# Hybrid decoder layer on one core: both feed-forwards begin with four plain hidden chunks instead of two, and the bias of x is added piece by piece inside the second norm

## What is computed

```
def _swiglu(x, w_gu, w_down):
    gate, up = jnp.split(x @ w_gu, 2, axis=-1)
    return (jax.nn.silu(gate) * up) @ w_down

h = _layernorm(ALPHA * x + 0.5 * _swiglu(x, p['ffa_w_gu'], p['ffa_w_down']), p['ln1_g'], p['ln1_b'])
...
h = _layernorm(ALPHA * h + mix, p['ln2_g'], p['ln2_b'])
y = _layernorm(ALPHA * h + 0.5 * _swiglu(h, p['ffb_w_gu'], p['ffb_w_down']), p['ln3_g'], p['ln3_b'])
```

## Time and profile before

| | us |
|---|---|
| median of 3 runs | 1262.5 (1261.45 to 1262.73) |
| the profiled execution, its own time | 1261.35 |
| its span (first to last instruction) | 1259.6 |
| TensorE busy | 1197.3 |
| VectorE busy | 842.0 |
| ScalarE busy | 498.2 |

### The profile page before, as it was taken

How to read it: one execution, slowest core, us unless ns; L and a number is a source line. 1 busy time by engine, 2 the same in 40 slices (tenths; PEclk the granted TensorE clock), 3 DMA queues, 4 the chain that set the end, 5 groups by cost and what they waited for, 6 DMA issues and landing times.

```text
span 1259.6 us, 30052 instructions
## 1 busy us (share of the span) xinstructions
PE 1197.3 (95%) x12778; PEld 1076.6 (85%) x12778; DVE 842.0 (67%) x1187; ACT 498.2 (40%) x759; POOL 89.7 (7%) x89
## 2 busy tenths in 40 slices
PE   9899999999999999998888988999799999999996
PEld 7899999999999988885546445698689999999996
DVE  6985895798467445164645543787796698579854
ACT  5441443254244325233433424333643244225433
POOL 0000000000020200000540021010000000000011
PEclk9999999999999999999999999999899999999998
DMA  5233222232315657646654898741123232422311
GB/s 206 98 96 123 101 93 93 101 107 95 112 63 178 237 169 250 219 143 200 220 175 154 272 301 286 255 169 60 42 97 94 102 120 68 132 95 101 101 34 69
DMA packets 56726, 177.41 MB, mean 141 GB/s; under 512 B 7185, under 2 KB 7442, under 8 KB 47250
## 3 DMA queue, kind: packets, MB, share of 16 engines
q1 hardware_dynamic: 53426, 169.48, 39.4%
q10 hardware_dynamic: 3168, 6.02, 1.4%
HBM read 164.64 MB, written 10.83 MB: 139 GB/s over the span
## 4 chain that ended last, share of the span: by engine, by line
PE 77%; DVE 10%; SPq 4%; issue 3%; DMA 2%; ACT 2%; POOL 1%; ACTq 0%; DVEq 0%; POOLq 0%
PE banks L585 30%; PE banks L385 30%; SPq L3057 2%; PE banks L1970 2%; PE banks L1227 2%; PE banks L408 2%; PE banks L977 2%; PE banks L1522 1%; PE banks L2040 1%; SPq L3049 1%; PE banks L2235 1%; DVE y_sum L1161 1%; DVE weights_lo L364 1%; DVE x_sums_lo L506 1%; PE banks L2227 1%
## 5 line engine op out<-in xcount | busy, mean ns | idle before, releaser
L364 DVE TENSOR_TENSOR weights_lo<-weights_raw,weights_hi 128x1024 fp32r<-128x1024 f32 (+1 forms) x82 | 96.5, 1183 | 119.7 <-ACT weights_hi L356 119.2
L356 ACT ACTIVATE weights_hi<-weights_raw 128x1024 fp32r<-128x1024 f32 (+1 forms) x82 | 82.4, 1013 | 189.8 <-PE banks L385 172.5
L385 PE MATMUL banks<-hidden_hi,weights_hi 128*128 128x260 f32 x576 | 116.3, 283 | 0.0
L385 PE MATMUL banks<-hidden_hi,weights_lo 128*128 128x260 f32 x576 | 115.5, 282 | 0.0
L385 PE MATMUL banks<-hidden_lo,weights_hi 128*128 128x260 f32 x576 | 115.5, 282 | 0.0
L585 PE MATMUL banks<-x_sums_hi,more_weights_hi 128*128 128x260 f32 x352 | 100.4, 285 | 0.7 <-DVE more_weights_lo L561 0.7
L585 PE MATMUL banks<-x_sums_hi,more_weights_lo 128*128 128x260 f32 x352 | 99.9, 284 | 0.0
L585 PE MATMUL banks<-x_sums_lo,more_weights_hi 128*128 128x260 f32 x352 | 99.9, 284 | 0.0
L385 PEld LDWEIGHTS banks<-hidden_hi,weights_hi 128*128 128x128 f32 x576 | 88.7, 188 | 0.3
L385 PEld LDWEIGHTS banks<-hidden_hi,weights_lo 128*128 128x128 f32 x576 | 88.7, 188 | 0.0
L385 PEld LDWEIGHTS banks<-hidden_lo,weights_hi 128*128 128x128 f32 x576 | 88.5, 188 | 0.0
(11 more groups left out here) (412 smaller groups left out, 3188.0 us busy)
## 6 DMA issues: line engine op xcount, KB each, us to landing
cache_pages<-in_cache_k SPq DMA_DIRECT2D x128, 256.0 KB, 3.6
weights_raw<-in_gate_up_b SPq DMA_DIRECT2D x22, 1024.0 KB, 4.7
weights_raw<-in_gate_up_a SPq DMA_DIRECT2D x21, 1024.0 KB, 4.7
cache_pages<-in_cache_v SPq DMA_DIRECT2D x64, 256.0 KB, 3.6
weights_raw<-in_w_in SPq DMA_DIRECT2D x13, 1024.0 KB, 6.3
projected<-in_cache_v SPq DMA_DIRECT2D x48, 256.0 KB, 3.6
weights_raw<-in_down_a SPq DMA_DIRECT2D x8, 896.0 KB, 4.5
weights_raw<-in_down_b SPq DMA_DIRECT2D x8, 896.0 KB, 4.6
```

What stands on the lines that cost most here:

```text
L356: nc.scalar.activation(WH[pr.slot(i, k)][:, 0:nk, :], RAW[slot][:, 0:nk, P * (k % 2):P * (k % 2) + P], ACT.Copy).then_inc(split_hi, 1)
L364: nc.vector.tensor_tensor(WL[pr.slot(i, k)][:, 0:nk, :], RAW[slot][:, 0:nk, P * (k % 2):P * (k % 2) + P], WH[pr.slot(i, k)][:, 0:nk, :].bi ...
L385: mm = nc.tensor.matmul(acc[s][:, a, 0:HALF], w[slot][:, t, :], x[:, k0 + t, HALF * a:HALF * a + HALF], start=begins and t == tiles[0] and ...
```

## The change

`PLAIN` becomes `(4, 4)`, one number for each feed-forward. `up_a` and `up_b` run twice, so that each feed-forward begins with four plain chunks and has three pairs left in its first group. For this case there is a new order of ACT's and DVE's lists, `longer_begin_scalar` and `longer_begin_vector`, which weaves the second plain product, the sums of x and the first pair's weights. The sums of x are rounded in the order 0, 1, 2, 3 rather than 1, 2, 0, 3. In the second norm `plain_x_scalar` adds the bias to one piece of `y_sum` at a time: three pieces after the norm's fourth `biased_scalar`, then one behind each, the last after the norm. The first sum of x, which reads the chunks 0 to 3 alone, waits for seven pieces, the others for all eleven.

```diff
-PLAIN = 2
+PLAIN = (4, 4)
...
-    def feed_forward(up, pair0):
+    def feed_forward(u, up, pair0):
...
-            first = PLAIN if not at else 0
+            first = PLAIN[u] if not at else 0
...
-    up_a = Product(PAIR_BODY, 1)
-    sevens_a, downs_a = feed_forward(up_a, 0)
+    up_a = Product(PAIR_BODY, PLAIN[0] // 2)
+    sevens_a, downs_a = feed_forward(0, up_a, 0)
...
-    up_b = Product(PAIR_BODY, 1, outp, LATE_RING)
-    sevens_b, downs_b = feed_forward(up_b, FC - PLAIN)
+    up_b = Product(PAIR_BODY, PLAIN[1] // 2, outp, LATE_RING)
+    sevens_b, downs_b = feed_forward(1, up_b, FC - PLAIN[0])
...
+        X_PIECES = ((0, 0), (1, 0), (2, 0), (0, 1), (1, 1), (2, 1), (3, None), (4, None), (5, None), (6, None), (7, None))
...
-        def plain_x_scalar(act):
-
-            act.wait_ge(x_ready, DC + 22)
-            for c in range(DC):
-                bias = VEC[:, V_LN + 3 * DC + c:V_LN + 3 * DC + c + 1]
-                nc.scalar.activation(Y[:, c, :], Y[:, c, :], ACT.Identity, bias=bias).then_inc(g("x_passes"), 1)
+        def plain_x_scalar(act, e):
+
+            c, h = X_PIECES[e]
+            act.wait_ge(x_ready, DC + 11 + e + 1)
+            bias = VEC[:, V_LN + 3 * DC + c:V_LN + 3 * DC + c + 1]
+            out = Y[:, c, :] if h is None else Y[:, c, HALF * h:HALF * h + HALF]
+            nc.scalar.activation(out, out, ACT.Identity, bias=bias).then_inc(g("x_passes"), 1)
 
         def x_sum_vector(dve, u, n):
 
             out = XS[:, n, :, :]
             if u:
-                dve.wait_ge(g("x_passes"), 4 + DC)
+                dve.wait_ge(g("x_passes"), 4 + (7 if n == 0 else len(X_PIECES)))
...
-        def plain_silu_scalar(act, up, k):
-            act.wait_ge(slab_used, up.slab(0, k) + 1)
+        def plain_silu_scalar(act, up, i, k):
+            act.wait_ge(slab_used, up.slab(i, k) + 1)
+            if i:
+                act.wait_ge(acc_free[2 + k], up.set_uses(i - 1, k + 2) + 1)
             nc.scalar.activation(halves(SCR[:, k, :]), accv(k), ACT.Silu).then_inc(acc_free[k], 1)
...
+        def longer_begin_scalar(act, up, u, sv):
+            for k in range(2):
+                split_high(act, up, 1, k)
+                plain_silu_scalar(act, up, 0, k)
+                x_sum_high(act, u, k)
+            for k in range(2, 4):
+                split_high(act, up, 1, k)
+            for n in range(2, 4):
+                x_sum_high(act, u, n)
+            for c in range(2):
+                plain_high_scalar(act, up, 0, c)
+            outer_high(act, sv, 0)
+            for k in range(2):
+                plain_silu_scalar(act, up, 1, k)
+            for which in ("first", "last"):
+                sums_high(act, sv, 0, which)
+            for c in range(2):
+                plain_high_scalar(act, up, 1, c)
+
+        def longer_begin_vector(dve, up, u, sv):
+            for k in range(2):
+                x_sum_vector(dve, u, k)
+            split_low(dve, up, 1, 0)
+            plain_hidden_vector(dve, up, 0, 0)
+            split_low(dve, up, 1, 1)
+            plain_hidden_vector(dve, up, 0, 1)
+            for n in range(2, 4):
+                x_sum_vector(dve, u, n)
+            for k in range(2, 4):
+                split_low(dve, up, 1, k)
+            for n in range(2):
+                x_sum_low(dve, u, n)
+            for c in range(2):
+                plain_low_vector(dve, u, 0, c)
+            outer_sums_vector(dve, sv, 0)
+            whole_sum_vector(dve, sv, 0)
+            outer_low(dve, sv, 0)
+            for n in range(2, 4):
+                x_sum_low(dve, u, n)
+            for which in ("first", "last"):
+                sums_low(dve, sv, 0, which)
+            plain_hidden_vector(dve, up, 1, 0)
+            outer_sums_vector(dve, sv, 1)
+            whole_sum_vector(dve, sv, 1)
+            plain_hidden_vector(dve, up, 1, 1)
+            for c in range(2):
+                plain_low_vector(dve, u, 1, c)
+
...
+
+        def feed_forward_scalar(act, up, u, sevens, downs):
+            if up.times > 1:
+                longer_begin_scalar(act, up, u, sevens[0])
+            else:
+                begin_scalar(act, up, u, sevens[0])
...
-        def norm_scalar(act, n, following=None):
+        def norm_scalar(act, n, following=None, plain=False):
...
                 biased_scalar(act, n, e)
                 if following and e == 4:
                     split_high(act, following, 0, 3)
+                if plain:
+                    for before in range(3) if e == 3 else (e - 1,):
+                        plain_x_scalar(act, before)
...
-            load_weights(sp, up_b, 0, by_pair(gu_b))
+            for i in range(up_b.times):
+                load_weights(sp, up_b, i, by_pair(gu_b))
...
-            norm_scalar(act, 1, up_b)
-            plain_x_scalar(act)
+            norm_scalar(act, 1, up_b, True)
+            plain_x_scalar(act, len(X_PIECES) - 1)
...
             multiply_halved(pe, up_b, 1)
+            for i in range(1, up_b.times):
+                multiply(pe, up_b, i, XH, XL)
```

More of the change, by code:

```diff
@@ L426, in layer @@
         COMBINE = {"second": 1, "third": 2, "ends": 3, "gates": 4, "hidden": 5}
-        X_STEP = {("sum", 0): 1, ("sum", 1): 2, ("sum", 2): 3, ("sum", 3): 4, ("low", 1): 5, ("low", 2): 6, ("low", 0): 7, ("low", 3): 8}
-        X_PASS = {1: 1, 2: 2, 0: 3, 3: 4}
+        X_STEP = ({("sum", 0): 1, ("sum", 1): 2, ("sum", 2): 3, ("sum", 3): 4, ("low", 1): 5, ("low", 2): 6, ("low", 0): 7, ("low", 3): 8},
+                  {(what, n): 4 * (what == "low") + n + 1 for what in ("sum", "low") for n in range(4)})
+        X_PASS = ({1: 1, 2: 2, 0: 3, 3: 4}, {0: 1, 1: 2, 2: 3, 3: 4})
         WEIGHT_AT = {4: 0, 1: 1, 2: 2, 5: 3, 6: 4, 7: 5, 3: 6}
@@ L456, in x_step @@
         def x_step(u, kind, n):
-            return 8 * u + X_STEP[kind, n]
+            return 8 * u + X_STEP[PLAIN[u] > 2][kind, n]
         def x_part(c, h):
@@ L756, in feed_forward_scalar, with begin_vector @@
             sums_high(act, sv, 0, "last")
-            for c in range(PLAIN):
-                plain_high_scalar(act, up, u, c)
+            for c in range(2):
+                plain_high_scalar(act, up, 0, c)
+        def begin_vector(dve, up, u, sv):
+            x_sum_vector(dve, u, 0)
+            x_sum_vector(dve, u, 1)
+            outer_sums_vector(dve, sv, 0)
+            whole_sum_vector(dve, sv, 0)
+            x_sum_vector(dve, u, 2)
+            x_sum_vector(dve, u, 3)
+            outer_low(dve, sv, 0)
+            sums_low(dve, sv, 0, "first")
+            plain_hidden_vector(dve, up, 0, 0)
+            for n in (1, 2):
+                x_sum_low(dve, u, n)
+            plain_hidden_vector(dve, up, 0, 1)
+            sums_low(dve, sv, 0, "last")
+            for n in (0, 3):
+                x_sum_low(dve, u, n)
[3 more added lines that the diff above has]
+            whole_sum_vector(dve, sv, 1)
@@ L769, in feed_forward_vector @@
         def feed_forward_vector(dve, up, u, sevens, downs):
-            sv = sevens[0]
-            x_sum_vector(dve, u, 0)
-            x_sum_vector(dve, u, 1)
-            outer_sums_vector(dve, sv, 0)
-            whole_sum_vector(dve, sv, 0)
-            x_sum_vector(dve, u, 2)
-            x_sum_vector(dve, u, 3)
-            outer_low(dve, sv, 0)
-            sums_low(dve, sv, 0, "first")
-            plain_hidden_vector(dve, up, u, 0)
-            for n in (1, 2):
-                x_sum_low(dve, u, n)
-            plain_hidden_vector(dve, up, u, 1)
-            sums_low(dve, sv, 0, "last")
-            for n in (0, 3):
-                x_sum_low(dve, u, n)
-            for c in range(PLAIN):
-                plain_low_vector(dve, u, c)
-            outer_sums_vector(dve, sv, 1)
-            whole_sum_vector(dve, sv, 1)
+            if up.times > 1:
+                longer_begin_vector(dve, up, u, sevens[0])
+            else:
+                begin_vector(dve, up, u, sevens[0])
             for n, (sv, down) in enumerate(zip(sevens, downs)):
@@ L3075, in _ @@
             sp.dma_start(RAW[1][:, :, :], by_pair(gu_a)(0, 1)).then_inc(raw_ready[1], 16)
+            for i in range(1, up_a.times):
+                load_weights(sp, up_a, i, by_pair(gu_a))
             load_feed_forward(sevens_a, downs_a, gu_a, down_a)
@@ L3220, in _ @@
             multiply(pe, up_a, 0, XH, XL, (x_ready, 0))
+            for i in range(1, up_a.times):
+                multiply(pe, up_a, i, XH, XL)
             feed_forward_tensor(pe, 0, sevens_a, downs_a)
@@ L3272, in by_pair, with gate_up @@
         return w[0].reshape(DC, P, -1, 2 * P).transpose(2, 1, 0, 3).reshape(-1, P, DC * 2 * P)
-    def gate_up(w):
+    def gate_up(w, plain):
         whole = w[0].reshape(DC, P, 2, FC // 2, 2 * P).transpose(3, 2, 1, 0, 4).reshape(FC, P, DC * 2 * P)
```

48 lines of the change are left out of this document (30 added, 18 removed).

## The result

The changed kernel takes 1245.76 us (median of 4 runs, 1240.84 to 1248.71), the kernel before beside it 1261.97 (1259.47 to 1262.73). The ratio is 0.9871, with a 95% interval of 0.9844 to 0.9899: faster by 1.0 to 1.6%. The median lies 0.9 us under the lower end of the predicted range, 1246.7. The profiled execution took 1248.23, its span is 1246.4; from the profiled execution before that is 13.1 us (13.2 in span), against a forecast of 14.1.

What follows compares the result with a forecast made beforehand. TensorE's matmuls plus its stalls and slow stretches were taken to bound the kernel. First feed-forward -1.2 and second -12.9 (norm's +0.5 included) gave -14.1 us, a median of 1248.4; the 8-in-10 range was 1246.7 to 1253.

Steps and rivals of the forecast that it cites:

- What bounded the kernel: Whole kernel: TensorE, busy for 95% of the span, sets the time by its matmuls plus where it stands or runs slowly.
- S: Second feed-forward, end of first plain product to down product: 66.70 us before, forecast 53.8 with the norm's 0.5, -12.9.
- Where the 16.3 us were: Second feed-forward's loss over 420 matmuls: waits of 8.6 and 2.4 us, most of the rest the low clock.
- the two waits: TensorE in the second feed-forward: 8.6 us for the first pair's outer low weights, 2.4 for the second pair's sums.
- The lists keep up: VectorE and ScalarE ready before TensorE asks, so no stalls from first plain product to down product: 53.3 us per feed-forward.
- The tightest margin: Second feed-forward, second plain product's first slab: inputs ready at 894.4, TensorE asks at 895.6, 1.2 us.
- the smallest one of the pairs: First feed-forward, second pair: last sums of weights come at 66.0, asked for at 68.5, a margin of 2.5 us.
- The reason given for the clock: Second feed-forward: the clock fell only after TensorE had stood, so removing the waits removes the low clock.
- The norm, +0.5: Second norm: bias instructions on ScalarE delay its sixth piece by 0.54 us; +0.5 taken, bounds 0 and 1.7.
- N: Second norm, from its first matmul with x to slab 3: 10.34 us before, forecast about 0.5 longer.
- The table load: Before the second feed-forward's first Silu: 1.28 us by the row; the skill page's 1.38 draining would make the sum 0.2 higher.
- The sum, -14.1: Whole kernel: -1.2 first feed-forward, -12.9 second including the norm's +0.5; 1247.3 us for the profiled execution, 1248.4 for the median.

Runs made afterwards that it cites:

- bias in a block: Changed kernel with all eleven bias pieces after the second norm, none inside it; 1249.41 us, ratio 0.9885.
- the copies: Changed kernel with extra unread copies of one slab's split on ScalarE after the second norm; 1248.69 us with one, 1254.41 with four.
- bias behind the seventh piece: Changed kernel with the bias put two pieces at a time behind the norm's seventh to eleventh piece; 1247.66 us, ratio 0.9869.
- one copy more: Changed kernel with one unread copy of a slab's split ahead of ScalarE's first split after the second norm; 1248.69 us, ratio 0.9879.
- again: Changed kernel run once more without an edit; 1249.98 us, ratio 0.9878 against the kernel before.
- four and two: Changed kernel with PLAIN = (4, 2): four plain chunks in the first feed-forward, two in the second, bias piece by piece; 1257.29 us, ratio 0.9944.
- two and two: Changed kernel with PLAIN = (2, 2): two plain chunks in each feed-forward, the piecewise bias alone; 1260.27 us, ratio 0.9972.
- two and four: Changed kernel with PLAIN = (2, 4): two plain chunks in the first feed-forward, four in the second; 1249.6 us, ratio 0.9895.
- four copies: Changed kernel with four unread copies of a slab's split ahead of ScalarE's first split after the second norm; 1254.41 us, ratio 0.9938.

## Why the prediction came out as it did

**What bounded the kernel: right.** The bias took 5.0 us of S, and the longer plain product the other 8.4 (61.67 to 53.29), net of its 2.9 us of matmuls: together the 16.3 us. Taken in the other order, by the kernel with the bias in a block, they are 11.2 for the plain product and 2.2 for the bias.

**Where the 16.3 us were: right for the two waits, wrong for the rest.** The prediction says of what is left beside 8.6 and 2.4 that "most of the rest is the clock". The clock cost 1.4 us, behind the second wait. Behind the first gap it cost nothing: the next two products start 2.94 and 2.85 us apart in three profiles, one of them with the clock high, because VectorE's low parts come no sooner. The 2.9 us by which the two distances exceed the 1.44 us of a product each were VectorE's lateness, like the gap itself. The error did not move the sum, which took the stretch as a whole; it would have, had the change only kept the clock up.

**The lists keep up, 53.3 us in each feed-forward: right.** Measured 53.29 and 53.29. The tightest margin was put at 1.2 us, and is 1.1 by the trace and 0.9 by the copies; the smallest one of the pairs, put at 2.5, is 2.5. The reason given for the clock, that it "fell only after TensorE had stood", does not hold: in the first profile of the changed kernel it fell in the norm behind 0.7 us at most. It did hold high through both stretches without a wait.

**The norm, +0.5: right in kind, mis-sized by 0.1.** N went from 10.34 to 10.75 or 10.76 in the six profiles with this norm in which no low clock fell into it: +0.41. The sixth piece comes 8.55 us after the norm's first matmul with x in the second profile of the changed kernel, 8.12 before (876.13 - 868.01): 0.43 late, not 0.54. In ScalarE's timeline above a half piece follows after 0.40 us rather than 0.42, and the instruction behind the split after 0.95 (875.07 to 876.02) rather than 1.06.

**The table load: the row decides.** The Silu starts 1.29 us after the load's start (892.37, 893.66), and the instruction ahead ends at 892.35, 0.02 before it. The Trainium skill's page "ScalarE: Activation LUTs", section "What ACT_TABLE_LOAD costs", adds about 1.38 us of draining to a switch of set. No such time stands around this load in any of the ten traces (0.02 us ahead of it, 1.29 from its start to the Silu), and with it the margin of 0.9 us would not be there.

**The sum, -14.1: right for the stretches.** In the profile the stretches that the change touches give -1.2 - 13.4 + 0.4 = -14.2, if the norm is taken at its undisturbed +0.4. The rest of the profiled difference of -13.2 in span lies outside them or in the clock: +1.6 of low clock in the norm, -0.9 at the start, +0.3 elsewhere. The profiled time was forecast at 1247.3 and is 1248.2.

**What failed: the spread of the runs, a term of the range.** I closed the 8-in-10 range below at 1246.7, with "no delay in the norm, the lower end of the runs", and took that lower end from three runs that lay within 1.3 us. That three runs lay so close was chance, and I took it for the spread. Over all 33 runs of the kernel before, times go from 1256.9 to 1268.14, with a standard deviation of 2.9 us; the ten runs of the changed kernel go from 1240.84 to 1252.42, standard deviation 3.8. The first four happened to be low (median 1245.76), the next six high (1249.98); the median of the ten is 1248.5, where the forecast was 1248.4. The mean of four runs with that deviation has a standard error of 1.9 us (3.8 over the root of four), twice the 0.9 by which the result lies under the range. That the median of ten meets the forecast to 0.1 is luck too: its own error is over 1 us. By the means, 1262.8 and 1247.6, the change is worth 15.2 us, with a standard error of about 1.3 (3.8 over the root of ten, 2.9 over the root of 33). The forecast of 14.1 lies within that. The two kernels with the same lists but for 0.4 us or less (bias behind the seventh piece, one copy more) have medians of 1247.66 and 1248.69.

**Where the spread sits.** Part is shown: in stretches that the change does not touch. From slab 3 of the first norm to the common mark in the output product, the profiled executions took 440.46 us (before), 440.84 (after), 442.96 (again) and 446.18 (bias behind the seventh piece), with mean clocks from 383 us on of 0.99 down to 0.97; over all ten profiles it is 440.1 to 446.2. The clock does not tell all of it: with the bias in a block the stretch took 442.26 at a clock of 0.99. The second norm took 1.6 us more in one of seven profiles with the same norm, and the first norm, which no edit touches, 1.6 more in two of ten. Over 84 runs (those of the changed kernel, of all eight experiments and of the kernel before beside these), the time falls by 0.9 us for every 0.001 of mean clock, taken within each kernel's group of runs, with a correlation of -0.70. So the clock goes with the spread and does not account for all of it. Why the clock falls in one execution of the mixing stage and not in the next, and what makes the rest, was not tried and stays open.

**A smaller term was missing.** The first feed-forward's wait of 2.4 us draws low clock in one of the three profiles with two chunks there (56.56 against 54.46 and 54.64), which I counted at none because the one profile had none. Taking the wait away is then worth 3.3 us in place of 1.2. It may be why the means give a little over 14.1; that is argued, not shown.

## What to carry to other kernels

A stage whose start is limited by preparation on other engines can be fed with costlier work that needs less preparation: here 24 more matmuls (2.9 us) of each feed-forward bought back the lateness of VectorE's list, 8.4 us net in the second. Before counting a low clock as a loss of its own, look whether the instructions behind it would have been ready sooner: here 2.9 us that looked like the clock's were VectorE's. Walk each engine's list in order with durations from the trace and compare with when TensorE asks: the walk gave 53.3 us and a margin of 1.2, the chip 53.29 and 0.9. Take the range from many runs, or from how the clock varies in the stages that are not touched: three runs within 1.3 us said nothing of a spread of over 10.

## What the runs showed of the hardware

Waits of TensorE of like length are not always followed by low clock. The feed-forwards of the ten profiles have these waits over 1.5 us, all with TensorE's clock high before:

| wait of TensorE | followed by low clock | not followed |
|---|---|---|
| 1.9 us | | bias in a block |
| 2.4 us | before (second feed-forward), four and two, two and two (both feed-forwards) | before (first feed-forward), two and four |
| 3.3 us | four copies, two and two | four and two |
| 8.6 us | before | |

It also fell once behind idle times of 0.7 us at most, in the norm of the first profile of the changed kernel (clock 0.86 in the 11 us of the window above), and not in six other profiles with the same norm. At the low clock a matmul of 260 columns goes in every 0.216 us, at the high one every 0.120, and the low stretch lasted some 12 to 27 matmuls. Such a stretch costs 1.4 to 2.8 us where TensorE's inputs are ready (1.4 behind the second wait of before, 2.8 with four copies), and nothing where they are not (the first pair of before and of two and two).
